# Each weight product of a two-block transformer kernel issued as two products of half the columns

## The reference

```python
h = _rms_norm(x, norm_g);  u = h @ w_in                      # 2048 x 6144
y = _depthwise_causal_conv(a * jax.nn.sigmoid(b), dw_w, dw_b)
x = x + (silu(layer_norm(y)) * silu(z)) @ w_out              # 2048 x 2048
kv = _rms_norm(x, kv_norm_g) @ w_kv                          # 2048 x 4096
u = _rms_norm(x, norm_g) @ w_in                              # 2048 x 4096 (q, z)
x = x + (rms_norm(diff_attention(q, k, v)) * silu(z)) @ w_out # 2048 x 2048
proj = rms_norm(x, pre_norm_w) @ w_in                        # 2048 x 5952
q_full = rms_norm(c_q, q_norm_w) @ w_q_up                    # 512 x 1536
kv = rms_norm(c_kv, kv_norm_w) @ w_kv_up                     # 256 x 2048
y = mixed @ w_out;  x = x + rms_norm(y, post_norm_w)         # 2048 x 2048
```

## Time and profile before

| | |
|---|---|
| time, median of 2 runs | 1340.66 us (1340.25 to 1341.08) |
| time of the profiled execution | 1340.45 us |
| its span, first to last instruction | 1338.7 us |
| PE (products) busy | 1306.9 us, 98% |
| PEld (loads of the stationary operand) busy | 1033.3 us, 77% |
| DVE, ACT busy | 841.1 us, 773.8 us |
| DMA, mean busy share of the 16 engines | 55% by queue 1, 170 GB/s |

### The profile page before, as it was taken

How to read it: one execution, slowest core, us unless ns; L and a number is a source line. 1 busy time by engine, 2 the same in 40 slices (tenths; PEclk the granted TensorE clock), 3 DMA queues, 4 the chain that set the end, 5 groups by cost and what they waited for, 6 DMA issues and landing times.

```text
span 1338.7 us, 15974 instructions
## 1 busy us (share of the span) xinstructions
PE 1306.9 (98%) x5864; PEld 1033.3 (77%) x5864; DVE 841.1 (63%) x1320; ACT 773.8 (58%) x1287; POOL 6.1 (0%) x51
## 2 busy tenths in 40 slices
PE   5999999999999999999999999999999999999996
PEld 4775555557888888888888887888988888888885
DVE  3679999987655665445575675555734444566544
ACT  3677888866545655444456565446754445566542
POOL 1000000000000000000000000000000000000000
PEclk9899999999999999999999999999999999999998
DMA  6555445555565655666654445565655556654563
GB/s 209 156 158 171 144 159 169 159 180 167 189 189 186 189 182 184 199 190 191 186 156 143 150 142 169 184 189 159 188 157 158 157 157 173 183 167 155 176 198 113
DMA packets 119567, 228.62 MB, mean 171 GB/s; under 512 B 7467, under 2 KB 11685, under 8 KB 119333
## 3 DMA queue, kind: packets, MB, share of 16 engines
q1 hardware_dynamic: 119460, 227.62, 55.2%
q10 hardware_dynamic: 32, 0.01, 0.0%
HBM read 225.50 MB, written 2.10 MB: 170 GB/s over the span
## 4 chain that ended last, share of the span: by engine, by line
PE 92%; ACT 3%; DVE 2%; DMA 1%; issue 1%; SPq 1%; DVEq 0%; ACTq 0%
PE PS L1349 24%; PE PS L1347 24%; PE PS L1348 24%; PE PS L1335 11%; PE PS L1265 3%; PE PS L1279 2%; DMA w_raw<-in_a_w_in 1%; ACT w_hi L403 1%; ACT L391 1%; DVE heads_out L1155 0%; DVE w_lo L833 0%; SPq L304 0%; ACT work L640 0%; ACT stage L456 0%; DVE aux L1235 0%
## 5 line engine op out<-in xcount | busy, mean ns | idle before, releaser
L833 DVE TENSOR_TENSOR w_lo<-w_raw,w_hi 128x1024 fp32r<-128x1024 f32 (+2 forms) x386 | 466.4, 1210 | 424.1 <-ACT w_hi L403 422.9
L403 ACT ACTIVATE w_hi<-w_raw 128x1024 fp32r<-128x1024 f32 (+2 forms) x386 | 403.4, 1047 | 424.3 <-PE PS L1349 388.4
L1347 PE MATMUL PS<-w_hi,actA_hi 128*128 128x512 f32 (+1 forms) x776 | 313.8, 404 | 10.7 <-DVE actA_lo L849 7.2
L1347 PE MATMUL PS<-w_hi,actB_hi 128*128 128x512 f32 (+1 forms) x768 | 304.8, 397 | 0.0
L1349 PE MATMUL PS<-w_hi,actA_lo 128*128 128x512 f32 (+1 forms) x776 | 302.5, 390 | 0.0
L1348 PE MATMUL PS<-w_lo,actA_hi 128*128 128x512 f32 (+1 forms) x776 | 302.0, 389 | 0.0
L1349 PE MATMUL PS<-w_hi,actB_lo 128*128 128x512 f32 (+1 forms) x768 | 297.8, 388 | 0.0
L1348 PE MATMUL PS<-w_lo,actB_hi 128*128 128x512 f32 (+1 forms) x768 | 296.9, 387 | 0.0
L1347 PEld LDWEIGHTS PS<-w_hi,actA_hi 128*128 128x128 f32 x776 | 146.7, 189 | 44.9 <-issue 9.2
L1348 PEld LDWEIGHTS PS<-w_lo,actA_hi 128*128 128x128 f32 x776 | 146.9, 189 | 32.8 <-issue 5.0
L1349 PEld LDWEIGHTS PS<-w_hi,actA_lo 128*128 128x128 f32 x776 | 146.6, 189 | 30.0
(11 more groups left out here) (204 smaller groups left out, 701.3 us busy)
## 6 DMA issues: line engine op xcount, KB each, us to landing
w_raw<-in_a_w_in SPq DMA_DIRECT2D x96, 512.0 KB, 4.1
w_raw<-in_w_in SPq DMA_DIRECT2D x88, 512.0 KB, 3.7
w_raw<-in_w_kv SPq DMA_DIRECT2D x64, 512.0 KB, 3.7
w_raw<-in_b_w_in SPq DMA_DIRECT2D x64, 512.0 KB, 3.7
w_raw<-in_a_w_out SPq DMA_DIRECT2D x32, 512.0 KB, 4.7
w_raw<-in_b_w_out SPq DMA_DIRECT2D x32, 512.0 KB, 3.7
w_raw<-in_w_out SPq DMA_DIRECT2D x32, 512.0 KB, 4.2
w_raw<-in_w_q_up SPq DMA_DIRECT2D x8, 384.0 KB, 3.4
```

The source lines that it names most:

```text
L403: nc.scalar.activation(w_hi[:, n % PARTS, 0:2 * w], w_raw[:, u % RAW, 0:2 * w], ACT.Copy)\
L833: V.tensor_tensor(w_lo[:, n % PARTS, 0:2 * w], w_raw[:, u % RAW, 0:2 * w], w_hi[:, n % PARTS, 0:2 * w].bitcast(F32), ALU.subtract)\
L1347: T.matmul(bank, ah, wh[:, kk, :], start=first and kk == 0, stop=False)
```

## The change

Each of the products of a weight unit is issued twice, once for each half of the columns, with the same stationary operand, into the two halves of the same bank. The widths become 256, 192 (of 384) and 160 (of 320). The number of product calls in `products` goes from 12 to 24 for a unit and from 4 to 8 for a whole one. Columns, operands, banks, semaphores and everything on the other engines stay. The first product of a bank alone carries `start`, the last alone `stop`.

```diff
                 first, last = i == 0, i == len(kts) // 2 - 1
+                halves = [slice(0, w // 2), slice(w // 2, w)]
                 if WHOLE[u]:
...
                         for tok in range(TT):
-                            ins = T.matmul(chunk_bank(c, tok), x_t[:, k, tok * P:(tok + 1) * P],
-                                           raw[:, kk, :], start=first and kk == 0, stop=last and kk == 1)
+                            for n, cols in enumerate(halves):
+                                ins = T.matmul(chunk_bank(c, tok)[:, cols], x_t[:, k, tok * P:(tok + 1) * P],
+                                               raw[:, kk, cols], start=first and kk == 0 and n == 0,
+                                               stop=last and kk == 1 and n == 1)
...
-                            T.matmul(bank, ah, wh[:, kk, :], start=first and kk == 0, stop=False)
-                            T.matmul(bank, ah, wl[:, kk, :], start=False, stop=False)
-                            ins = T.matmul(bank, al, wh[:, kk, :], start=False, stop=last and kk == 1)
+                            for m, (a, b) in enumerate(((ah, wh), (ah, wl), (al, wh))):
+                                for n, cols in enumerate(halves):
+                                    ins = T.matmul(bank[:, cols], a, b[:, kk, cols],
+                                                   start=first and kk == 0 and m == 0 and n == 0,
+                                                   stop=last and kk == 1 and m == 2 and n == 1)
```

## The result

The changed kernel takes 1402.88 us (median of 2, 1402.72 to 1403.04) against 1340.66. The ratio is 1.0464, 95% interval 1.0419 to 1.0509: slower by 62.2 us. The forecast was 1412 us, range 1398 to 1468.

A forecast was written before the change was run, and what follows sets the result against it. The prediction took PE as the bound almost from end to end. Wide products 58.7, narrow chunks 12.3 and whole units 0.3 sum to 71.3 us, on 1340.66 giving 1412 us, range 1398 to 1468.

The forecast's parts named there:

- What bounds the kernel: PE is the bound almost from end to end, standing still 5.4 us in all from 52 to 1330 us.
- Wide products: 512-column fp32r products: halving adds a second fixed part of 13.4 ns to each of 4380, +58.7 us.
- Loads: Loads of the stationary operand set a floor of 112 ns; 256-column halves at 120 keep them hidden, margin 8 ns.
- rival (b): Load floor and fixed part add to 125.4 ns a half, 1467 us; chance 0.13 with what lies between.
- (c): A load holds its unit for its 189 ns record, about 2044 us; chance 0.03 with other pitches above 126 ns.
- Narrow chunks: Halves of the 384- and 320-column products fall below the load floor and take 112 ns each, +12.3 us.
- Whole units: 336 float32 records of 429 ns become 672 of 215, +0.3 us.
- After short groups: Some ten products behind such a group have steps of 230 to 240 ns; left at 0, doubled 3 us more.
- Waits: ACT, DVE and SP gain slack as a unit lasts 2.88 us in place of 2.72; no wait moves onto PE.
- (a): Only 2 ns of the fixed cost belong to each fp32r product, 1362 us; chance 0.09 with its neighbourhood.

The follow-up runs named there:

- e3: The changed kernel with the halves outermost, the three products of a half next to one another; 1403.26 us, ratio 1.0466.
- e5: The kernel before, products in one piece, token half innermost, so that each product goes to the other bank than the one before it; 1340.25 us, ratio 0.9998.
- e9: The kernel before, products in one piece, with only 64 of each 128 tokens stationary in about 7/8 of the fp32r products; 1349.46 us, ratio 1.0066.
- e6: The kernel before with the hi and lo parts of weights and activations in bfloat16 in place of fp32r; 1290.93 us, ratio 0.9629.
- e8: e6 with each weight product in four quarters (128, 96 and 80 columns), whole units in one piece; 1326.38 us, ratio 0.9894.
- e2: The kernel before with only the 192 products of 384 and 320 columns halved; 1352.93 us, ratio 1.0092.
- e7: e6 with every weight product halved, narrow ones too, whole units in one piece; 1301.94 us, ratio 0.9711.
- e4: The kernel before with only the 512-column products cut, into 384 + 128 columns; 1592.0 us, ratio 1.1876.
- e1: The kernel before with only the fp32r products of 512 columns halved; 1389.8 us, ratio 1.0368.
- e10: e4 with half of the columns in the load of about 7/8 of the products, the other tokens' sums incomplete; 1399.19 us, ratio 1.0438.

## Why the prediction was right, point by point

**What bounds the kernel.** Right. Behind the start PE stands still for 5.4 us before and 4.6 after. ACT and DVE did the same work in the longer time and held nothing more up.

**Wide products.** Right in mechanism and size. The pitch is 120.0 ns (120.1 forecast); 4380 x 13.3 = 58.4 us (58.7). That the fixed part doubles is shown by 120.0 at 256 columns on the line through 320, 384 and 512; that it comes with each fp32r product, whether the operand or the bank changes or not, by e3 and e5; that a shorter load doesn't lower it, by e9; that it is gone in the bfloat16 kernels, by e6 to e8. In every run each product has a load of its own. So the runs can't tell a cost of the product from one of the same size for each load, whatever the load's length. What in the fp32r path takes the 13.3 ns is not shown.

**Loads.** The floor is real and was placed well: 112 ns taken, 111.7 and 112.7 measured. The wide halves lie above it. The margin of 8 ns held, and floor and fixed part don't add, so rival (b) is out; (c) is out by the 96% that the load records now fill without holding anything up.

**Narrow chunks.** 12.3 us forecast. The steps of these products sum to 43.1 us after and 31.1 before, +12.0; e2 measured +12.6 by itself.

**Whole units.** 0.3 forecast, 0.8 by the steps (139.4 us for 646 steps of 215.8 after, 133.0 for 310 of 429.2 before).

**After short groups.** This is the term that was mis-sized, and the largest part of why 71.3 came out as 62.2. I left the excess behind such groups as it was, and named 3 us more as the bound. It fell away. To measure it, each record of the trace before is set beside the one or two that answer to it after. From the second step behind a transposed or attention group or a whole unit on, without steps that hold a wait and without the first 54 us, the products grew by 4.2 us less than 13.3 ns each: **-4.2 us** where the sum had 0. (With the full-clock part of the start, the steps of 512 columns lie 3.5 us over 226.7 each, those of 256 columns 1.1 us under 120.0.) I had put the sign on the wrong side without a reason that excluded a gain. In e6 the timeline behind such a group has no excess either.

**Waits.** The prediction said that no wait would move onto PE, and put nothing down for the waits that were there. They shrank. PE's list of waits sums to 20.1 us before and 18.1 after. The middle of the kernel has these before and then after:

```profile
PE PS L1459 <- DVE heads_out L1017: 0.9, 1, 0.9
PE PS L1265 <- DVE heads_out L1155: 0.7, 1, 0.7
PE PS L1275 <- DVE heads_out L1043: 0.5, 3, 0.2
PE PS L1418 <- DVE work L1037: 0.3, 1, 0.3
```
```profile
PE PS L1464 <- DVE heads_out L1017: 0.8, 1, 0.8
PE PS L1265 <- DVE heads_out L1155: 0.4, 1, 0.4
```

Behind 54 us seven steps hold a wait. Together they grew by 2.0 us less than 13.3 ns each.

**The rest.** The same comparison gives -1.0 us for the first step behind short groups and whole units, -1.1 for the last step before them and -0.5 for the short products themselves. The first 54 us give +0.1: 50 of the 4380 wide products lie there, with 0.7 of cost, and waits and half clock are shorter (after the long wait some seven pairs of halves go at half clock, where before twelve whole products do). The other 4330 cost 57.6. So 57.6 + 12.0 + 0.8 - 4.2 - 2.0 - 1.0 - 1.1 - 0.5 + 0.1 = 61.7, and the traces differ by 1383.6 - 1321.8 = 61.9 us from the start of the first product to that of the last. Why the first and the last step shrink is not shown.

**Rivals.** (a), that only 2 ns belong to a product, had 0.09 and the row of the float32 chain for it; e3 and the 120.0 refute it for fp32r. For bfloat16 a fixed part of about 2 ns is what the runs show: e7 over e6 is +0.9%.

## What to carry to other kernels

When PE is the bound, cost a split by the pitch and not by busy time: take the steps of one type at two or three widths, and the intercept is the price of every further product; here 13.3 ns for fp32r and 2.5 for bfloat16. Then look for the floor that the load of the stationary operand sets, 109 to 113 ns for 128 fp32r columns: at 256 moving columns it is hidden, at 192, 160 and 128 each product costs the floor, and an uneven cut is worse than an even one (e4 against e1, 202 us). In this kernel every way of cutting a product that fits a bank cost time.

## What was not expected of the hardware

- Behind a group of short products the steps of 512-column fp32r products are 224 to 236 ns for about ten products, mostly over their steady 226.7, those of 256 columns 117 to 121, mostly under their steady 120.0. The bfloat16 kernel has none of it: 6 rows behind such a group, from 999.96 to 1001.04, are 216 ns apart. In e9, with the shorter fp32r load, such steps fill the whole run (225, 226, 234, 230, 236 and 229 ns, over and over). So it was seen with fp32r alone, and the length of the load has a part in it. The cause stays open; no run here moves a load against its product by itself.
- In e10 a pair of 384 and 128 columns takes 235 ns, 213.3 by its columns and 22 more, where two fixed parts would be 26.6. So the fixed part isn't the same for every pair of widths once the load is halved. Which of the two products has less of it can't be read from the steps of 176 and 60 ns, since e4 shows that a step can hold what belongs to its neighbour.
- At half clock 512 fp32r columns take 427 ns and 256 take 213, columns alone. The 13.3 ns appear only at 2.4 GHz. Why, these runs can't tell.
